# The last 12 expert-key blocks in rounded parts, the gate batches packed three to two blocks, and half of their gated rows made on ScalarE

## The reference

```
q = (xt @ wq).reshape(n, 8 heads, 2, 128);  s = einsum(q, subkeys)
top 16 of each side, top 16 of the 16 x 16 sums  -> eidx, cs
gate = softmax(cs)
hid = gelu(einsum('cd,chkd->chk', x, u[eidx]))
out = einsum('chk,chkd->cd', gate * hid, v[eidx])
```

## Time and profile before

| | |
|---|---|
| three runs | 1794.41, 1795.15, 1796.36 us |
| profiled execution, first to last instruction (span) | 1793.2 us |
| PE / DVE / ACT / POOL busy | 99% / 77% / 43% / 10% |
| first u stage | 516 to 901 us |
| first v stage | 901 to 1195 us |
| second u stage | 1195 to 1487 us |
| second v stage and end | 1487 to 1793 us |

### The profile page before, as it was taken

How to read it: one execution, slowest core, us unless ns; L and a number is a source line. 1 busy time by engine, 2 the same in 40 slices (tenths; PEclk the granted TensorE clock), 3 DMA queues, 4 the chain that set the end, 5 groups by cost and what they waited for, 6 DMA issues and landing times.

```text
span 1793.2 us, 27943 instructions
## 1 busy us (share of the span) xinstructions
PE 1774.3 (99%) x10680; PEld 1591.7 (89%) x10680; DVE 1388.5 (77%) x2153; ACT 766.7 (43%) x1054; POOL 170.8 (10%) x158
## 2 busy tenths in 40 slices
PE   8999999999999999999999999999999999999998
PEld 8899989789999999999977777789999998777775
DVE  6546667566459796888378898989999998898996
ACT  5334444655331010111155555555555555555555
POOL 0000000000000121222100000111111111111010
PEclk9999999999999999999999999999999999999999
DMA  9774544556545987998999899999999999999984
GB/s 351 262 280 149 165 141 142 188 187 226 187 150 192 358 333 282 342 336 331 362 377 361 317 324 341 344 350 367 377 369 374 377 347 361 353 359 365 357 309 152
DMA packets 77275, 531.01 MB, mean 296 GB/s; under 512 B 8811, under 2 KB 9211, under 8 KB 16268
## 3 DMA queue, kind: packets, MB, share of 16 engines
q1 hardware_dynamic: 54512, 377.96, 56.6%
q0 software_dynamic: 22352, 151.59, 23.2%
q10 hardware_dynamic: 332, 0.44, 0.1%
HBM read 512.60 MB, written 15.20 MB: 294 GB/s over the span
## 4 chain that ended last, share of the span: by engine, by line
PE 97%; DVE 1%; issue 1%; ACT 1%; DMA 0%; DVEq 0%; SPq 0%; ACTq 0%
PE bank L918 19%; PE bank L934 11%; PE bank L596 8%; PE bank L597 8%; PE bank L598 8%; PE bank L1015 6%; PE bank L1014 6%; PE bank L1019 6%; PE bank L1021 6%; PE bank L1020 6%; PE bank L935 5%; PE bank L973 2%; PE bank L743 0%; PE bank L952 0%; PE bank L791 0%
## 5 line engine op out<-in xcount | busy, mean ns | idle before, releaser
L1932 DVE TENSOR_TENSOR lo<-raw,hi 128x1024 fp32r<-128x1024 f32 x384 | 463.6, 1221 | 101.7 <-ACT hi L1318 101.3
L1318 ACT ACTIVATE hi<-raw 128x1024 fp32r<-128x1024 f32 x384 | 404.9, 1059 | 320.8 <-PE bank L1021 233.5
L918 PE MATMUL bank<-hT,raw 128*128 128x192 f32 x2048 | 337.4, 326 | 0.0
L918 PEld LDWEIGHTS bank<-hT,raw 128*128 128x128 f32 x2048 | 332.3, 190 | 0.1
L934 PE MATMUL bank<-xr,hi 128*128 128x384 f32 x1024 | 291.3, 359 | 0.0
L935 PE MATMUL bank<-xr,lo 128*128 128x192 f32 x1024 | 256.3, 250 | 0.0
L1444 DVE TENSOR_TENSOR lo<-raw,hi 128x2048 fp32r<-128x2048 f32 x75 | 171.8, 2290 | 103.7 <-ACT hi L1086 68.2
L1015 PE MATMUL bank<-lo,wm 128*64 128x512 f32 x512 | 202.8, 396 | 0.0
L1014 PE MATMUL bank<-hi,wm 128*128 128x512 f32 x512 | 199.9, 390 | 1.7 <-DVE wm L1987 1.2
L1019 PE MATMUL bank<-lo,wm 128*128 128x512 f32 x512 | 200.3, 391 | 0.0
L1021 PE MATMUL bank<-hi,wm 128*128 128x512 f32 x512 | 199.3, 389 | 0.0
(11 more groups left out here) (293 smaller groups left out, 2686.2 us busy)
## 6 DMA issues: line engine op xcount, KB each, us to landing
raw<-in_u SPq DMA_DIRECT2D x128, 1024.0 KB, 7.7
raw<-in_v SPq DMA_DIRECT2D x128, 1024.0 KB, 7.2
raw<-in_w_in SPq DMA_DIRECT2D x43, 1024.0 KB, 5.8
raw<-in_w_out SPq DMA_DIRECT2D x16, 1024.0 KB, 4.8
raw<-in_wq SPq DMA_DIRECT2D x16, 1024.0 KB, 4.8
gate_matrix<-gs POOLq DMA_DIRECT2D x12, 768.0 KB, 12.5
gs<-gate_matrix SPq DMA_DIRECT2D x12, 768.0 KB, 9.2
raw<-in_cmp_w SPq DMA_DIRECT2D x8, 1024.0 KB, 4.8
```

The costliest lines, as they stand in the source:

```text
L918: last = mm(bank[s % 2][:, 0:TD], raw[:, s, k * P:(k + 1) * P], xn[:, k, 0:TD], start=(k == 0), stop=(k == KT - 1))
L1318: do(hi[:, s % 2, cols], raw[:, s, cols], ACT.Copy).then_inc(v_hi_ready, 1)
L1932: vec.tensor_tensor(lo[:, n % 2, cols], raw[:, n % RAW, cols], hi[:, n % 2, cols].bitcast(F32), ALU.subtract).then_inc(v_lo_ready, 1)
```

## The change

It does four things.

1. The last 12 u blocks of the first half (52 to 63) become split blocks. `xr` is therefore made at the end of the native blocks and no longer in the v stage: five parts after block 50, eleven after block 51. PE waits for it part by part within block 52.
2. The 24 gate batches are spread over 16 blocks (33 to 48) and no longer over 24. One batch follows an odd block and two follow an even one. The store of two batches stands in POOL's order four blocks after the second of them, as before.
3. Four of the eight gated one-hot tiles of each batch are made on ScalarE (`gated_rows_of`): Square of the difference, then Relu of gate - 2 x square, each Relu waiting for the instruction before it. In ACT's order they stand behind the evacuation of an earlier batch.
4. The gelus of the fetched rows come four blocks later on ACT. The first residual piece loads into a place of its own (`res_first`).

```
+EARLY_SPLIT = 12
+NATIVE = HALF - EARLY_SPLIT
+BATCHES, GATES_BY = TD // 8, ROUTED + 1 + 16
+def batches_by(r): return BATCHES * min(max(r - ROUTED, 0), GATES_BY - ROUTED - 1) // (GATES_BY - ROUTED - 1)
+def block_of_batch(b): return next(r for r in range(HALF) if batches_by(r) > b)
+ACT_ROWS = (4, 5, 6, 7)
...
 # POOL
-                if 6 <= r < 6 + BATCHES and r % 2 == 0:
-                    store_gates(r // 2 - 3)
+                for x in range(BATCHES // 2):
+                    if b == block_of_batch(2 * x + 1) + 4:
+                        store_gates(x)
...
 # PE
             def gate_batch(b):
                 pe.wait_ge(onehots_ready, b + 1)
+                pe.wait_ge(act_rows_ready, 2 * len(ACT_ROWS) * (b + 1))
                 if b >= 2:
                     pe.wait_ge(gate_evac, b - 1)
                     pe.wait_ge(gate_applied, b - 1)
...
-            for r in range(GATE_BLOCKS):
-                u_block(ROUTED + r, (ROUTED + r) % RAW)
-                if 1 <= r <= BATCHES:
-                    gate_batch(r - 1)
+            for r in range(ROUTED, NATIVE):
+                u_block(r, r % RAW)
+                for b in range(batches_by(r - 1), batches_by(r)):
+                    gate_batch(b)
+            for r in range(EARLY_SPLIT):
+                u_split_block(r, r % RAW, half=0, opening=(r < 2))
...
 # ACT
+            def gated_rows_of(b):
+                if b >= 2:
+                    ac.wait_ge(gate_rows, b - 1)
+                for x in ACT_ROWS:
+                    t, row = 8 * b + x, onehot[:, b % 2, 1, x, :]
+                    do(row, iota, ACT.Square, bias=choiceT[:, 1, t:t + 1], scale=-1.0).then_inc(act_rows_ready, 1)
+                for n, x in enumerate(ACT_ROWS):
+                    t, row = 8 * b + x, onehot[:, b % 2, 1, x, :]
+                    ac.wait_ge(act_rows_ready, 2 * len(ACT_ROWS) * b + len(ACT_ROWS) + n)
+                    do(row, row, ACT.Relu, bias=choiceT[:, 2, t:t + 1], scale=-2.0).then_inc(act_rows_ready, 1)
...
             for r in range(1, HALF):
+                if r in (NATIVE - 2, NATIVE - 1):
+                    round_split(r - NATIVE + 2)
+                if r > NATIVE:
+                    round_split(r - NATIVE + 1)
...
+                if r == NATIVE - 2:
+                    for k in range(5):
+                        spread_xn(k)
+                if r == NATIVE - 1:
+                    for k in range(5, KT):
+                        spread_xn(k)
...
-                if ROUTED + 2 <= r < ROUTED + 2 + BATCHES:
-                    gate_copy(r - ROUTED - 2)
+                if r > ROUTED:
+                    for b in range(batches_by(r - 1), batches_by(r)):
+                        if b >= 1:
+                            gate_copy(b - 1)
+                        if b + 1 < BATCHES and b >= batches_by(ROUTED + 1) - 1:
+                            gated_rows_of(b + 1)
...
 # DVE
-                items_to(items_by(ROUTED + b - 1))
+                items_to(items_by(block_of_batch(b) - 2))
             apply_gates(BATCHES - 1)
-            items_to(items_by(HALF - 1))
+            items_to(items_by(NATIVE - 4))
...
+            for x in range(2):
+                for part in range(2):
+                    rest_split(x, part)
+                for k in range(*((0, 5), (5, KT))[x]):
+                    spread_rest(k)
+            for x in range(2, EARLY_SPLIT):
+                rest_split(x, 0)
+                sum_u(NATIVE + x - 2, half=0)
+                rest_split(x, 1)
+                items_to(items_by(NATIVE + x - 1))
```

More of the change, by code:

```diff
@@ L112, in gelus_at, with seen @@
 def gelus_at(b):
-    return [q for q in range(PAIR_TILES // GROUP) if items_by(b - 1) >= group_end(q) > items_by(b - 2)]
+    def seen(b):
+        return items_by(b - 1 - (GELU_LAG if b < HALF - 4 else 0))
+    return [q for q in range(PAIR_TILES // GROUP) if seen(b) >= group_end(q) > seen(b - 1)]
 def group_end(q):
     return ITEMS.index(("u", GROUP * q + GROUP - 1)) + 1
+GELU_LAG = 4
 SBUF_0 = 16512
@@ L919, in u_block, with u_split_block @@
                 last.then_inc(block_done, 1)
-            def u_split_block(r, s, opening=False):
-                if opening:
+            def u_split_block(r, s, half=1, opening=False):
+                done = 2 * (EARLY_SPLIT + HALF) if half else 0
+                if opening and half:
                     pe.wait_ge(half_kept, r + 1)
-                    pe.wait_ge(xr_lo, KT)
+                elif opening:
+                    pe.wait_ge(acc_evacuated, M_PEER + NATIVE + r - 1)
                 else:
-                    pe.wait_ge(u_summed, r - 1)
+                    pe.wait_ge(u_summed, r + ((EARLY_SPLIT if half else 0) - 1))
                 acc_bank = bank[s % 2]
@@ L930, in u_split_block @@
                     if k % 8 == 0:
-                        pe.wait_ge(v_hi_ready, 2 * r + (2 * HALF + k // 8 + 1))
-                        pe.wait_ge(v_lo_ready, 2 * r + (2 * HALF + k // 8 + 1))
+                        pe.wait_ge(v_hi_ready, 2 * r + (done + k // 8 + 1))
+                        pe.wait_ge(v_lo_ready, 2 * r + (done + k // 8 + 1))
+                    if opening and not half and r == 0:
+                        pe.wait_ge(xr_lo, k + 1)
                     w = slice(k * P, (k + 1) * P)
@@ L984, in _ @@
                     for b in range(2, 8):
-                        last = mm(bank[b][:, :], hi[:, 0, 0:P], hi[:, 0, 0:512], start=True, stop=True)
+                        last = mm(bank[b][:, :], xr[:, 0, 0:P], xr[:, 0:2, :].rearrange("p k n -> p (k n)")[:, 0:512], start=True, stop=True)
                     last.then_inc(banks_opened, 1)
@@ L1285, in hidden_block, with hidden_gelu @@
                 do(hidden[:, r * TD:(r + 1) * TD], bank[r % 2][:, 0:TD], ACT.Gelu_apprx_tanh).then_inc(acc_evacuated, 1)
-            def hidden_gelu(r):
-                ac.wait_ge(u_summed, r + 1)
+            def hidden_gelu(r, half=1):
+                ac.wait_ge(u_summed, r + 1 + (EARLY_SPLIT if half else -NATIVE))
                 cols = hidden[:, r * TD:(r + 1) * TD]
@@ L1903, in onehots @@
                                   choiceT[:, 0, 8 * b:8 * b + 8].unsqueeze(2).to_broadcast([P, 8, P]), ALU.is_equal)
-                for t in range(8 * b, 8 * b + 8):
+                for t in (8 * b + x for x in range(8) if x not in ACT_ROWS):
                     last = vec.tensor_scalar(onehot[:, b % 2, 1, t % 8, :], iota, choiceT[:, 1, t:t + 1], choiceT[:, 2, t:t + 1],
@@ L1969, in _ @@
                                           ALU.mult).then_inc(gated, 1)
[L1970 to L1978 removed]
+                    rest_split(EARLY_SPLIT + 2 * HALF * half + mv, 0)
+                    if mv < 2:
+                        sum_u(HALF - 2 + mv, half)
+                    rest_split(EARLY_SPLIT + 2 * HALF * half + mv, 1)
                     if half and mv in (HALF - 16, HALF - 15):
```

99 lines of the change are left out of this document (45 added, 54 removed).

## The result

The changed kernel takes **1905.53 us** (median of 5 runs, 1904.78 to 1909.36), against 1795.15 us. The ratio is 1.0618 (95% interval 1.0606 to 1.0631). The span of the profiled execution is 1903.0 us, 109.8 more than before. The direction and the mechanism came out as forecast; the size did not: 1873 us was forecast, with 1900 as the upper end.

What follows compares the result with a forecast made beforehand. PE was taken to bound the kernel. Stops of 80.7 us, less 7.8 saved and a 0.3 gap, gave +72.6; with 5 for the clock, 78 on 1793.2, and 2 for timed runs: 1873 us, range 1848 to 1900.

Steps and rivals of the forecast that it cites:

- What PE saves: Twelve u blocks made split: each takes 4.55 us instead of 5.20, saving 7.8 us.
- the opening: Start of the split (rounded) blocks: PE waits for parts of `xr` made by ACT and DVE in turn, 3.0 us.
- The chain behind the store: Gate part: DVE item, fetch, store landing, evacuation 4, 14.9 us after batch 5; with rows, PE stops about 12 us.
- the price of the rows: Four Squares and four Relus on ACT behind the evacuation, before batch 6 may start: 1.9 us, bounds 1.0 and 2.8.
- the clock: PE at half clock after five stops over 9 us: 1.8 us each, 9 at most, 5 us taken.
- The rounded blocks: Losses in the twelve split blocks, from parts of `xr` and waits for items: 21.1 us.
- the three waits for items: Split blocks: four DVE items in a row wait for fetches; block 55 stops 11.0 us, block 56 4.0; 18.1 in all.
- Stores in time: Rival: gate stores land in time, leaving late rows, the opening and DVE's four items; 1810 us, chance 0.06.
- All hidden: Rival: split blocks' saving is real and ACT's rows finish within the batch ahead, unseen by PE; 1790 us, chance 0.04.
- Longer landings with the full clock: Rival: same mechanism with median landings, each stop 2.5 to 3 us longer, full clock loss; 1898 us, chance 0.12.
- The bound of +64 us: Walk of all batches with the shortest landings, 9.6 us for a store and 5.6 for a fetch: +64 us.
- the walk of the order before: Same step-by-step walk of the unchanged kernel: no stop of PE, four ACT waits for stores of 1.4 to 1.6 us.

Runs made afterwards that it cites:

- experiment 9: As experiment 8, with 14 items up to block 59, 37 in the first v stage, none on DVE behind the last rounded block: 1792.47 us.
- Experiment 1: The changed kernel with each gate store two blocks behind its second batch in POOL's order, not four: 1839.92 us.
- Experiment 4: The changed kernel with 90 thrown-away products on PE in front of the stopped batches, block 51 and the fourth rounded block: 1892.4 us.
- Experiment 3: The changed kernel with DVE taking one fetched item per rounded block instead of four in a row at once: 1901.15 us.
- experiment 8: As experiment 5, with 16 items up to block 59, 35 in the first v stage, evenly spread over rounded blocks, none at the first v block: 1793.62 us.
- experiment 6: The changed kernel with stores two blocks behind, all gated rows on DVE and one item per rounded block: 1804.07 us.
- experiment 5: The changed kernel with stores two blocks behind their batches and all gated rows on DVE: 1812.2 us.

## Why the prediction was right and where it was wrong

**What PE saves: right.** The saving is real and small. With all stops of the gate part gone and nearly all of the rounded blocks', the time ends 2.3 us below the kernel before (experiment 9), with 2.1 us of the opening (3.0 forecast) and 1.5 around the wait for a part of `u` still in it.

**The chain behind the store: right.** Its place, its links and its length to the start of the evacuation (14.95 us for 14.9) stand in the chain above, and the landing taken (9.95 us) is the measured median. ACT's waits are 87.0 us where near 79 were forecast. Experiment 1 moves only the stores, and the long stops go. Item 18's fetch is the third in the POOL order and not the fourth; the chain is not touched by it.

**The step that failed first: the price of the rows.** The prediction took 1.9 us between bounds of 1.0 and 2.8. Measured are 1.16 for the four Squares and 4 x 0.43 for the Relus, in all 2.98 us to PE's start. A Relu that waits for the instruction before it on its own engine starts 0.43 us after it; 0.3 was taken. The measured value lies just beyond the upper bound, since the rows behind the bound are of instructions that wait for nothing on their own engine, and the range carried the term at one value. It returns in every stop: the short ones are 2.33 us and not 1.2, the long ones 1 to 2 us longer (block 51's 2.7). Together these are the 15.1 us of the table, though other links of the chains may be in it too.

**The step that failed most: the clock.** The prediction counted five long stops at 1.8 us at most, and took 5 us for all. Lost are 21.8, of these 17.4 in front of the rounded blocks and 4.4 in them. A long stop costs 2.0 to 2.9 us, not 1.8: the products at the program's start reached the full pace 4.55 us after the first, and here PE ran for 4 us at 0.50 and 3 more at 0.68. And short stops cost as well, where the clock falls behind them: 3.23 us for a batch instead of 2.02, and with the next block some 1.65 in all. The price was put on stops over 9 us alone, a limit for which no row of before spoke; the earlier trace rows showed only that the clock fell within 8.2 idle us. Experiment 4 shows the cause by itself. The Trainium skill, "TensorE: Matmul & The Clock Gate", section "Why this matters for your kernels", says that idle gaps of PE between bursts bring the half clock back. The trace agrees at the long stops: 0.50 behind the 13.18 us. Here the clock fell behind some stops of 2.33 us as well.

**The rounded blocks: the size about right by luck, the account of it only in part.** 22.8 us are lost where 21.1 were forecast. But the three waits for items are 15.5 and not 18.1, and the 4.4 at the lower clock, which the sum had elsewhere, fill the gap. Of the waits, 13.83 us stand in front of the fourth block (11.0 forecast), while DVE waits for the third and the fourth item of the row:

```profile
956.17 2.29 DVE L1846 SCALAR_TENSOR_TENSOR rows_sb<-rows_sb,xs 128x2048 f32<-128x2048 f32 x1 [8.87 <-DMA rows_sb<-in_u_rows,pairs]
...
960.63 2.29 DVE L1846 SCALAR_TENSOR_TENSOR rows_sb<-rows_sb,xs 128x2048 f32<-128x2048 f32 x1 [2.15 <-DMA rows_sb<-in_u_rows,pairs]
```

But the four in a row are not the root of most of it. Experiment 3 takes them apart and wins 4.4 us only: fetches still land late, and DVE, which needs 5.00 us for a rounded block with an item where PE needs 4.55, has no lead that would cover them. The prediction never set these two against each other. Experiments 8 and 9 take items out of the stretch, and the waits fall from 7.9 us (experiment 6) to 1.7 and 1.3. Fewer items relieve DVE and the fetches at once, so they don't say which of the two counts for more.

**The rivals.** Stores in time was put at 1810. Experiment 1 is that case made on purpose and takes 1840, since the late rows cost twice what was written, the clock falls behind some of them, and the items' stop is 16.9 us. All hidden was put at 1790; experiment 9, in which nearly all is, has 1792.5. Longer landings with the full clock, at 1898, came closest in time and was wrong in its cause, since the landings were short. The range failed because it was made from the landings: the rows stood in it at 1.9 us throughout, and the clock at 9 us at most where 21.8 were lost.

**Sums in the prediction that don't hold.** The bound of +64 us gives 1793.2 + 64 + 2 = 1859 us, not the 1848 at which the range begins. And the walk of the order before gave ACT four waits of 1.4 to 1.6 us, about 6 in all, where the trace has 12.3; that was a sign that the walk read the waits too short, and it was not followed up.

**Left open.** Why the clock falls behind some stops of 2.33 us and not behind others, no run tells. Nor does one tell whether the 0.43 us are the semaphore's or the write's. Why the load of one part of `u` comes late in experiments 6, 8 and 9 was not gone after.

## What to carry to other kernels

When the users of a ring of buffers are packed more densely, the place at which each buffer is emptied must move with them: count for every wait which block the release stands behind and which block needs it. Price a chain of small instructions that wait for one another by dependent ones, or keep both ends in the range, and give the work behind a stop of PE a price at half the clock, short stops included. Where another engine gets a task per block, add up its whole block against PE's, and when the transfers that it needs can land, before its order is looked at.

## What the runs showed of the hardware that was not expected

- The granted clock was 1.00 through a stop of 2.33 us (728.6 to 731.0) and 0.60 in the 3 us of dense products behind it. Behind another stop of 2.33 us (experiment 1, batch 5) the batch took 2.02 us, at the full pace, and behind the next 3.40. The loss has two sizes only: of the eight short stops of experiment 1, six cost 1.5 to 1.7 us in the batch and block behind them, and two nothing. In the changed kernel it is three of five stops of that length, at 1.6 to 1.7 us.
- The same holds at the opening of the rounded blocks, where PE waits four times for 0.24 to 0.27 us. In the changed kernel and in experiment 6 six pairs of products behind these waits start 0.53 us apart and not 0.285, in experiments 3, 5, 8 and 9 none do.
- ScalarE starts Squares of 128x128 that wait for nothing every 0.29 us, and Relus of that size that each wait for the one before every 0.43 us.
- The landing of a store hangs on what was issued just ahead of it. POOL's timeline in the changed kernel and in experiment 9 (start, us, instruction, idle before):

```profile
737.98 1.18 POOL L566 DMA_INDIRECT rows_sb<-in_v,pairs  x1 [11.62 <-DVE acc L1849]
739.16 1.12 POOL L573 DMA_DIRECT2D gate_matrix<-gs  x1
```

```profile
764.93 1.03 POOL L573 DMA_DIRECT2D gate_matrix<-gs  x1 [5.94 <-ACT gs L1360]
```

In the first the store starts with the 1 MB fetch just issued and lands after 9.95 us; over all twelve its kernel has 9.7 to 14.5. In the second no fetch stands nearer than 7.3 us ahead of a store, and the landings are

```profile
DMA to landing us min/median/max: 5.0/5.9/6.9
```

A fetch behind the store does no such harm: eight of these twelve have one within 1.4 us behind them, DMA's share is up to 0.96 in the six microseconds from the issue, and they land after 5.0 to 6.9 us. Experiment 1 has both cases in one kernel: its two stores directly behind a fetch land after 9.1 and 9.6 us, those 2.9 to 3.5 us behind one after 7.4 to 8.9, and those over 6.5 us behind one after 5.1 to 6.3. Whether the fetch ahead holds the store in the queue or by its traffic was not taken apart.
